# Folding the sample tokens' small matmuls into every weight unit instead of every second one

## The reference

```
def mixer_sublayer(x, ...):
    xn = rms_norm(x, norm_g)
    proj = xn @ w_in                              # 1024 -> 5 * 1024
    u, v, xr, g_a, g_b = jnp.split(proj, SPLITS, axis=-1)
    v = layer_norm(jax.nn.gelu(v), ln_g, ln_b)
    y_a = chunk_spatial_gating(jax.nn.gelu(u), v, w_s, b_s)
    xc, new_buf = causal_depthwise_conv(xr, conv_buf, conv_w, conv_b)
    y_b, h_last = rg_lru(xc, h0, lam, w_a, b_a, w_x, b_x)
    merged = sigmoid(g_a) * y_a + sigmoid(g_b) * y_b
    return x + merged @ w_out, ...

def hier_moe(x, ...):      # 32 experts of width 256, the top 2 of one group of 8
    gates = ...            # group top-1, then expert top-2
    h = silu(x @ w_gate[e]) * (x @ w_up[e])
    return sum over e of gates * (h @ w_down[e])
```

## Time and profile before

| | us |
|---|---|
| median of 3 runs | 685.99 |
| lowest and highest | 684.7 and 688.97 |
| the profiled execution | 688.97 |
| its span in the trace | 687.3 |

### The profile page before, as it was taken

One profiled execution on the slowest core, in us unless ns is written; L12 is line 12 of the kernel. 1 busy time (PEld: TensorE's weight loads), 2 busy tenths in 40 slices (PEclk: granted clock), 3 DMA queues, 4 the chain that ended last, 5 costly groups with the idle time before them and its releaser, 6 DMA issues.

```text
span 687.3 us, 8484 instructions
## 1 busy us (share of the span) xinstructions
PE 563.1 (82%) x2668; PEld 341.4 (50%) x2668; DVE 294.7 (43%) x581; ACT 242.5 (35%) x386; POOL 65.0 (9%) x137
## 2 busy tenths in 40 slices
PE   3899799999999999999996069898998877777800
PEld 3576496777778778777663023333333323222200
DVE  4924637767768667666325801001100100000038
ACT  5422424465573663753236202222121211111122
POOL 1200070000000000000000011221221111110000
PEclk9999999999999999999999569999999999999965
DMA  8222233932222222322807569999999999998164
GB/s 311 85 84 100 76 123 118 379 100 69 85 73 93 69 69 92 99 61 103 333 1 272 224 231 420 422 420 419 420 421 420 421 421 420 422 421 350 50 235 164
DMA packets 32002, 156.33 MB, mean 227 GB/s; under 512 B 6160, under 2 KB 6544, under 8 KB 19312
## 3 DMA queue, kind: packets, MB, share of 16 engines
q1 hardware_dynamic: 25744, 143.10, 52.9%
q0 software_dynamic: 5472, 10.63, 4.2%
q10 hardware_dynamic: 768, 2.38, 0.9%
HBM read 150.82 MB, written 14.17 MB: 240 GB/s over the span
## 4 chain that ended last, share of the span: by engine, by line
PE 53%; DMA 15%; SPq 15%; DVE 10%; issue 3%; ACT 3%; POOLq 0%; POOL 0%; DVEq 0%; ACTq 0%
SPq L440 14%; PE ps L1189 13%; PE ps L1190 12%; PE ps L1191 12%; DMA wslot<-in_wmoe 4%; DMA xg<-xnd,colg 4%; DMA ytok<-yo,coly 4%; PE ps L1463 3%; PE ps L1442 2%; PE ps L1305 2%; PE ps L1337 2%; DVE x L1170 1%; PE ps L1431 1%; PE ps L1216 1%; PE ps L1289 1%
## 5 line engine op out<-in xcount | busy, mean ns | idle before, releaser
L1442 PE MATMUL ps<-wslot,xgT 128*64 128x512 f32 x528 | 124.1, 606 | 21.0 <-DMA wslot<-in_wmoe 18.0
L589 ACT ACTIVATE wh<-raw 128x1024 fp32r<-128x1024 f32 x48 | 50.8, 1059 | 167.5 <-PE ps L1191 117.7
L1189 PE MATMUL ps<-xh,wh 128*128 128x512 f32 x256 | 102.8, 402 | 0.0
L1190 PE MATMUL ps<-xh,wl 128*128 128x512 f32 x256 | 100.0, 391 | 0.0
L1191 PE MATMUL ps<-xl,wh 128*128 128x512 f32 x256 | 100.0, 391 | 0.0
L1145 DVE TENSOR_TENSOR hm<-hs,ps 128x256 f32<-128x256 f32 x17 | 7.2, 421 | 200.6 <-ACT hs L748 200.6
L1442 PEld LDWEIGHTS ps<-wslot,xgT 128*64 128x64 f32 x528 | 41.0, 139 | 101.3 <-issue 101.2
L774 DVE TENSOR_TENSOR wl<-raw,wh 128x1024 fp32r<-128x1024 f32 x48 | 58.6, 1223 | 59.8 <-ACT wh L589 58.9
L1463 PE MATMUL ps<-wslot,hT 128*64 128x512 f32 x264 | 65.5, 627 | 11.8 <-DMA wslot<-in_wmoe 6.1
L1189 PEld LDWEIGHTS ps<-xh,wh 128*128 128x128 f32 x256 | 48.2, 188 | 16.9 <-issue 7.5
L1191 PEld LDWEIGHTS ps<-xl,wh 128*128 128x128 f32 x256 | 48.2, 188 | 10.6
(11 more groups left out here) (288 smaller groups left out, 738.6 us busy)
## 6 DMA issues: line engine op xcount, KB each, us to landing
wslot<-in_wmoe SPq DMA_DIRECT2D x99, 1024.0 KB, 25.4
raw<-in_wmix SPq DMA_DIRECT2D x48, 512.0 KB, 3.9
gy<-ytok SPq DMA_DIRECT2D x8, 512.0 KB, 7.3
xt<-in_x SPq DMA_DIRECT2D x4, 512.0 KB, 7.1
x<-in_x SPq DMA_DIRECT2D x4, 512.0 KB, 5.1
xnd<-xn ACTq DMA_DIRECT2D x4, 512.0 KB, 9.2
out_y<-xn SPq DMA_DIRECT2D x4, 512.0 KB, 2.6
gw<-in_wgate POOLq DMA_DIRECT2D x8, 128.0 KB, 2.3
```

The source lines that it names most:

```text
L589: a.activation(wh[:, hslot, :], raw[:, slot, :, :].rearrange("p k c -> p (k c)"), ACT.Copy).then_inc(hi_ready, 1)
L1189: pe.matmul(out, sh, mh_, start=start, stop=False)
L1190: pe.matmul(out, sl, mh_, start=False, stop=False)
L1442: l = pe.matmul(ps[CAP * s:CAP * s + CAP, 2, :], xgT[:, c, CAP * s:CAP * s + CAP], wslot[q][s][:, c * 512:(c + 1) * 512], start=c == 0, st ...
```

## The change

The sample tokens' matmuls are issued in every unit, two at a time, instead of in every odd unit, four at a time. A unit's two blocks k go to two column positions: 0 and 32 in an even u, 64 and 96 in an odd u. There are 32 of them, as before (16 in the v projection, 16 in the output projection), but in 16 groups of two and not in 8 groups of four. As a unit is now read by nobody after its own end, SP waits for `unit_done >= n - 3` for every n.

```diff
             for n in range(4, 12):
                 e.wait_ge(lo_ready, n - 3)
-                e.wait_ge(unit_done, n - 3 + (n + 1) % 2)
+                e.wait_ge(unit_done, n - 3)
                 e.dma_start(raw[:, n % RAW, :, :], wmix[n]).then_inc(raw_in[n % RAW], 16)
...
             for n in range(44, 48):
                 e.wait_ge(lo_ready, n - 3)
-                e.wait_ge(unit_done, n - 3 + (n + 1) % 2)
+                e.wait_ge(unit_done, n - 3)
...
+                    wr_ = raw[:, slot, :, :].rearrange("p k c -> p (k c)")
                     for t in range(NT):
                         before(u, t)
...
-                            last = product(ps[:, banks[t], :], sth[:, k, tok], stl[:, k, tok], wh[:, n % 2, c], wl[:, n % 2, c],
-                                           k == 0, k == KT - 1)
+                            product(ps[:, banks[t], :], sth[:, k, tok], stl[:, k, tok], wh[:, n % 2, c], wl[:, n % 2, c],
+                                    k == 0, k == KT - 1)
                     before(u, NT)
-                    if u % 2:
-                        for q in range(4):
-                            k = 2 * u - 2 + q
-                            from_ = raw[:, (slot - 1 + q // 2) % RAW, :, :].rearrange("p k c -> p (k c)")
-                            last = pe.matmul(ps[S * q:S * q + S, sbank, :], sts[:, k, :], from_[:, q % 2 * 512:q % 2 * 512 + 512],
-                                             start=k < 4, stop=k >= 4, tile_position=(0, S * q), skip_group_check=True)
+                    for kk in range(2):
+                        k = 2 * u + kk
+                        q = k % 4
+                        last = pe.matmul(ps[S * q:S * q + S, sbank, :], sts[:, k, :], wr_[:, kk * 512:kk * 512 + 512],
+                                         start=k < 4, stop=k >= 4, tile_position=(0, S * q), skip_group_check=True)
                     last.then_inc(unit_done, 1)
                     after_unit(u)
```

## The result

The changed kernel takes 691.08 us (median of 5, 688.38 to 692.4) against 685.99; the ratio is 1.0069, with an interval from 1.0044 to 1.0096, so it is slower by 3.0 to 6.6 us. 690.7 was forecast. The profiled execution took 691.71 us, its span is 690.1; that is 2.7 us more than the profiled execution of before, for which 4.7 more was forecast.

The account below looks back on a forecast made before the run. PE's work was taken as the bound in the projections, with delays reaching the end: 688.97 + 7.8 (groups) - 1.4 (unit 11's load) - 1.7 (clock) = 693.7, +4.7; against the median 685.99, 690.7 us. Range 687.5 to 694.2.

Parts of the forecast that it names:

- The price of a group: Sample matmuls in both projections: a group of two costs as much as four, 1.20 us between fp32r matmuls.
- The output projection: Units 40 to 47: four new groups, so 4.4 us longer from unit 40's start to the first gather.
- It reaches the end: Experts start when the output projection's chain ends, so a microsecond there is a microsecond at the end.
- The v projection: Units 0 to 7: three new groups on the path, +3.4 us; unit 0's group hidden in PE's idle time.
- unit 11: Behind unit 7: unit 11's load goes out first and alone, so PE waits less, -1.4 us.
- The clock's term: V projection: the slow stretch at 36 to 42 us goes, -1.7 us; the one at 80 to 86 stays, 0.
- Rival 1: Both slow stretches' places: no clock comes back, +6.4 us, 692.4 us; chance 0.31.
- rival 2: Ahead of unit 2 and behind unit 7: both slow clock stretches go, +3.0 us, 689.0 us; chance 0.13.
- Rivals 3 and 4: Sample groups: 3, matmuls cost by the piece, 683.7 us (0.06); 4, a group's two don't overlap, 704.2 us (0.04).
- The unit loads: SP's earlier loads of units 4, 6, 8, 10, 44, 46: five worth nothing, unit 10's pays through unit 11.

Follow-up runs that it names:

- early-group kernel: Kernel before, with the groups of four moved from the odd unit's end to its start and SP waiting on their own semaphore: 681.06 us, ratio 0.9912.

## Why the prediction was right

**The price of a group** (1.20 between fp32r matmuls, two as dear as four): measured 1.20 and confirmed from both sides, with two in series (+0.85) and with four (+0.02 a unit). Beside `fold_rows` I took 1.00, and it is 0.89. That 0.20 of the 1.20 is lost on the way in and out is what the distances show; no run tells why.

**The output projection** (+4.4): +4.2 between the marks, in two pairs of traces. With the measured terms it is 2 x 1.20 + 0.89 + 0.98 = 4.3, and the small wait of 0.1 us ahead of unit 42 in the earlier trace rows is gone.

**It reaches the end:** yes. The experts' stage isn't shown to absorb any of it; with the new output projection alone the time is up by 3.6 to 7.1 us.

**The v projection** (+3.4 for the groups, -1.4 for unit 11, -1.7 for the clock, so +0.3): in the first pair of profiles it is 0.0 (96.09 against 96.06). From unit 2's start to unit 7's end the changed kernel takes 1.7 us more, which is +3.4 for the groups and -1.7 for the clock; from there to the first channel tile it takes 1.5 less, which is the load; and unit 2 starts 0.2 earlier. The first term holds where the clock stays up from 23 to 30 us; where it was slow all that time, the group behind unit 0 cost 1.14 more. The clock's term is the weak step: it was taken from one execution as if it were a property of the kernel. Second profiles gave the same stretch in the kernel before, and one slow stretch less in the changed kernel, but the kernel with the new v projection alone was +1.0 to +3.8, not within 1 throughout.

**The total:** +4.7 was forecast and 3.0 to 6.6 measured. Rival 1 (+6.4, no clock comes back) lies inside that interval too, and rival 2 (+3.0, both stretches go) at its lower end; the changed kernel's second profile looks like rival 2. So the terms in PE's work and in the load are shown; how much of the difference the clock gives back in the median is not settled by these runs, and that the total came within 0.4 us of the forecast is in part luck. The sum was made for the profiled execution, and there it came out at 691.71 and not at 693.7: up to the first rows it was 4.2 us later, for 4.7 forecast, but the experts' stage was 1.5 shorter. Rivals 3 and 4 are refuted.

**The unit loads:** as forecast, only unit 11's landing paid; the kernel with SP's old waits has the same time between the marks, so unit 46's early load did nothing.

## What to carry to other kernels

Where small matmuls share the array at different column positions, count groups, not matmuls: splitting a group of four into two groups of two doubled its cost, 1.2 us for each new group. The good half of such a change, freeing a buffer earlier, could be had here without the bad half, by moving the whole group ahead of the long work of its unit and giving it a semaphore of its own (-6 us instead of +5, of which 2.3 us are the wait that went). And a term that rests on where the clock fell in one profile needs a second profile before it goes into a sum.

## What the runs showed of the hardware that I had not expected

The clock's slow stretches ahead of `z_mixing` move from one execution to the next of the same kernel: the kernel before showed them at 37 and 81 us and at 36 and 77 us, of 3.4 and of 6.8 us length; the changed kernel at 81 us and not at all. In all kernels of this study PE does the same work until 26 us, with an idle time of 2.1 us that ends at 24.1 to 24.4. The clock stayed up through it in 9 of the 14 profiles (all four of the kernel before and the changed one among them), and in five it fell within it, at 23.4 to 23.8 us. The Trainium skill (TensorE: Matmul & The Clock Gate, "What's actually happening") says that what watches PE's activity runs freely and doesn't start anew with a kernel; that the stretches move between executions agrees with it. Where the clock was slow from 23 to 30 us, it took the idle time behind it away, so that an added group cost 1.14 us in one execution and was hidden in another.

The two kinds can be told apart before the hole. At the start PE's fp32r matmuls stand 0.43 us apart, and later 0.23. The step comes at 15.5 to 16.3 us in the nine profiles whose clock stayed up, and at 16.6 to 17.0 us in the five whose clock fell. Here it is in the kernel before (clock stayed up) and with the new v projection alone (clock fell):

```profile
15.52 0.63 PE L1189 MATMUL ps<-wh,xh 128*128 128x512 f32 x1
15.95 0.56 PE L1190 MATMUL ps<-wh,xl 128*128 128x512 f32 x1
16.34 0.40 PE L1191 MATMUL ps<-wl,xh 128*128 128x512 f32 x1
16.57 1.04 PE L1241 MATMUL ps<-ident,xt 128*128 128x128 f32 x8
...
15.49 0.63 PE L1189 MATMUL ps<-wh,xh 128*128 128x512 f32 x1
15.91 0.63 PE L1190 MATMUL ps<-wh,xl 128*128 128x512 f32 x1
16.34 0.55 PE L1191 MATMUL ps<-wl,xh 128*128 128x512 f32 x1
16.73 1.03 PE L1248 MATMUL ps<-ident,xt 128*128 128x128 f32 x8
```

That is a pattern in 14 profiles; no run sets the moment of the step on purpose.

Float32 matmuls of different lines run side by side as well: in the early-group kernel the first records of `fold_rows` and of L1307 start 0.24 us apart (75.75 and 75.99), each lasts 0.6 us, and the second record of `fold_rows` starts only at 76.18.
